# Expert blocks in quarters of the columns, with the activations turned by VectorE in 32x32 blocks

## The reference, cut to what matters

```python
def expert_block(args):
    xblk, e = args
    gu = xblk @ w_gu[e] + b_gu[e]                 # 1024 x 2048: gate | up
    gate, up = jnp.split(gu, 2, axis=-1)
    gate = jnp.minimum(gate, SWIGLU_LIMIT)
    up = jnp.clip(up, -SWIGLU_LIMIT, SWIGLU_LIMIT)
    act = (up + 1.0) * gate * jax.nn.sigmoid(SWIGLU_ALPHA * gate)
    return act @ w_down[e] + b_down[e]            # 1024 x 1024
```

## Time and profile before

| | us |
|---|---|
| median of 3 runs (lowest to highest) | 2428.33 (2425.53 to 2428.96) |
| the profiled execution, own time | 2426.65 |
| its span, first to last instruction | 2424.6 |
| outside the span | 2.05 |
| PE busy | 2286.5 (94%) |
| mean granted clock of TensorE, share of full | 0.974 |

### The profile page before, as it was taken

How to read it: one execution, slowest core, us unless ns; L and a number is a source line. 1 busy time by engine, 2 the same in 40 slices (tenths; PEclk the granted TensorE clock), 3 DMA queues, 4 the chain that set the end, 5 groups by cost and what they waited for, 6 DMA issues and landing times. The chain is left out here.

```text
span 2424.6 us, 40637 instructions
## 1 busy us (share of the span) xinstructions
PE 2286.5 (94%) x17071; PEld 1023.0 (42%) x17071; DVE 686.2 (28%) x1189; ACT 494.4 (20%) x908; POOL 93.7 (4%) x105
## 2 busy tenths in 40 slices
PE   5999869999999999999999993799999998999998
PEld 2434433444444444444444441346445444444443
DVE  1133455111111111111111115102066202365633
ACT  2211222111110111111110111101016202355530
POOL 0000000000000000000000003000000000000000
PEclk9999989999999999999999995899999999999999
DMA  9148439999999999999999965321220121222100
GB/s 352 52 154 310 158 135 382 399 390 392 378 403 397 391 393 393 395 392 390 394 392 398 384 254 174 139 80 70 87 79 8 44 78 44 69 87 87 69 35 35
DMA packets 142024, 561.61 MB, mean 232 GB/s; under 512 B 16217, under 2 KB 31730, under 8 KB 108082
## 3 DMA queue, kind: packets, MB, share of 16 engines
q1 hardware_dynamic: 118662, 512.67, 54.7%
q0 software_dynamic: 9520, 35.26, 4.6%
q10 hardware_dynamic: 13788, 12.93, 1.6%
HBM read 535.77 MB, written 25.03 MB: 231 GB/s over the span
## 5 line engine op out<-in xcount | busy, mean ns | idle before, releaser
L1759 PE MATMUL ps<-ring,xeT 128*32 128x512 f32 x4096 | 491.2, 597 | 2.9 <-ACT xeT L1480 2.9
L1763 PE MATMUL ps<-ring,xeT 128*32 128x256 f32 x4096 | 268.7, 380 | 0.0
L1735 PE MATMUL ps<-ring,aT 128*32 128x512 f32 x2048 | 267.5, 594 | 1.1 <-DVE aT L1638 1.1
L1763 PEld LDWEIGHTS ps<-ring,xeT 128*32 128x32 f32 x4096 | 133.1, 110 | 199.0 <-issue 155.0
L1759 PEld LDWEIGHTS ps<-ring,xeT 128*32 128x32 f32 x4096 | 126.7, 110 | 197.0 <-issue 160.3
L1625 DVE TENSOR_SCALAR gate<-ps 128x768 f32<-128x768 f32 x32 | 30.6, 958 | 547.1 <-PE ps L1763 547.1
L1569 ACT ACTIVATE sig<-gate 128x768 f32<-128x768 f32 x32 | 27.0, 845 | 729.6 <-DVE gate L1625 729.6
L358 PE MATMUL ps<-hT_late,ring 128*128 128x512 f32 x384 | 165.2, 592 | 1.3 <-PEq L1999 1.3
L1740 PE MATMUL ps<-ring,aT 128*32 128x256 f32 x2048 | 157.6, 379 | 0.0
L1740 PEld LDWEIGHTS ps<-ring,aT 128*32 128x32 f32 x2048 | 67.0, 110 | 152.7 <-issue 152.7
L358 PEld LDWEIGHTS ps<-hT_late,ring 128*128 128x128 f32 x384 | 72.9, 190 | 92.9 <-issue 92.9
(11 more groups left out here) (371 smaller groups left out, 2190.0 us busy)
## 6 DMA issues: line engine op xcount, KB each, us to landing
ring<-in_w_gu SPq DMA_DIRECT2D x256, 1024.0 KB, 7.1
ring<-in_w_down SPq DMA_DIRECT2D x128, 1024.0 KB, 7.9
ring<-in_even_w_in SPq DMA_DIRECT2D x18, 1024.0 KB, 6.2
ring<-in_w_ada SPq DMA_DIRECT2D x32, 512.0 KB, 6.4
ring<-in_odd_w_in SPq DMA_DIRECT2D x32, 512.0 KB, 5.3
ring<-in_w_ada SPq DMA_DIRECT2D x8, 1024.0 KB, 21.0
ring<-in_w_in SPq DMA_DIRECT2D x8, 1024.0 KB, 15.8
y_scratch<-ysb ACTq DMA_DIRECT2D x128, 64.0 KB, 4.9
```

Source lines behind the costliest of these rows:

```text
L1735: mm = nc.tensor.matmul(quad(Y0, 2 * q + n), acted(k, q), w[:, kk, n * BANK:(n + 1) * BANK], start=first, stop=last)
L1759: nc.tensor.matmul(quad(2 * b, 2 * q + h), left(q), w[:, at:at + BANK], start=start, stop=stop)
L1763: mm = nc.tensor.matmul(quad(2 * b + 1, c, 256), left(2), w[:, at:at + 256], start=start, stop=stop)
```

## The change

- **gate and up** go by quarters of the columns for all three groups. A quarter c is not a run of columns: `part_columns` takes from gate and from up, of each 128 columns, the 32 at place c, so a matmul streams 2 x 8 runs of 32 columns, 512 in all, which lie 128 apart. A tile has 12 matmuls of 512 columns, three rounds of four strips; group q is in bank q, gate in its first 256 columns, up in the next. Bank 3 is free.
- **The turn of the activations** is one `nc.vector.transpose` of 128x768 from `up` to `turned`, which turns each block of 32x32 where it is. With the new order of columns that gives what `down` needs. PE's 6 transposes and DVE's two copies go. The instruction waits for `down` of the expert before (`y_done`), since that reads `turned`.
- **ids** are written to bank 3 (`IDS`), and `pe_ids` moves from behind the first tile to the end of the step, with a third one before step 0. `down` doesn't wait for `ids_read` any more.
- **The turn of `xe`** has 96 tokens instead of 128, and so has ACT's `act_modulate`.
- **Empty slots** have the id 8192 (`NONE`) and are dropped by the bounds check of the gather; `xe` keeps there what it had.

The diff, cut to its core:

```diff
-        Y0 = 4
+        IDS, Y0 = 3, 4
...
         def dve_ids(dve, S):
-            nc.vector.tensor_scalar(idx[:], ps[:, Y0, 0:1], ps[:, Y0, 1:2], None, ALU.add).then_inc(S.ids_read, 1)
+            nc.vector.tensor_scalar(idx[:], ps[:, IDS, 0:1], ps[:, IDS, 1:2], float(NONE), ALU.add, ALU.add).then_inc(S.ids_read, 1)
...
-                mm = nc.tensor.transpose(ps[:, 6 + k // 4, (k % 4) * P:(k % 4 + 1) * P], src[:, k * P:(k + 1) * P], ident)
+                at = (k % 4) * P
+                mm = nc.tensor.transpose(ps[:, 6 + k // 4, at:at + tokens_], src[0:tokens_, k * P:(k + 1) * P],
+                                         ident[0:tokens_, 0:tokens_])
...
+        FQ = FF // 4
+        def part_columns(w, c):
+            return w.rearrange("p (b j c f) -> p c b j f", b=2, c=4, f=QUAD)[:, c]
+        def part_banks(b):
+            return ps[:, 0:3, b * FQ:(b + 1) * FQ]
...
-            nc.gpsimd.indirect_dma_start(xe[0:CAP, :], None, xn_dram, bass.IndirectOffsetOnAxis(ap=idx[0:CAP, :], axis=0)) \
-                .then_inc(S.gathered, 16)
+            nc.gpsimd.indirect_dma_start(xe[0:CAP, :], None, xn_dram, bass.IndirectOffsetOnAxis(ap=idx[0:CAP, :], axis=0),
+                                         bounds_check=T - 1, oob_is_err=False).then_inc(S.gathered, 16)
...
-                    dve.wait_ge(M.aT_done, e * 2 + 1)
-                    nc.vector.tensor_copy(turned[:, 0:BANK], bank(6)).then_inc(M.aT_read, 1)
-                    dve.wait_ge(M.aT_done, e * 2 + 2)
-                    nc.vector.tensor_copy(turned[:, Q2], bank(7, W - BANK)).then_inc(M.aT_read, 1)
+                    dve.wait_ge(M.act_ready, e + 1)
+                    if not first:
+                        dve.wait_ge(M.y_done, e * 2)
+                    nc.vector.transpose(turned[:, 0:W], up[:, 0:W]).then_inc(M.aT_read, 1)
...
-                for e in range(2):
+                for e in range(3):
...
-                    pe.wait_ge(M.ids_read, e + 3 if not (isinstance(e, int) and e == E) else E + 2)
                     pe.wait_ge(M.y_read, e * 2)
-                    pe.wait_ge(M.aT_read, e * 2)
+                    pe.wait_ge(M.aT_read, e)
...
-                    if q < 2:
-                        at = (k % 4) * P + q * 2 * QUAD + (k // 4) * QUAD
-                    else:
-                        at = BANK + (k % 2) * P + (k // 2) * QUAD
+                    at = q * FQ + k * QUAD
                     return turned[:, at:at + QUAD]
...
-                    for b in range(2):
-                        for q, h in pair_units():
-                            at = b * FF + h * BANK
-                            nc.tensor.matmul(quad(2 * b, 2 * q + h), left(q), w[:, at:at + BANK], start=start, stop=stop)
-                    for b in range(2):
+                    for q in range(3):
                         for c in range(4):
-                            at = b * FF + c * 256
-                            mm = nc.tensor.matmul(quad(2 * b + 1, c, 256), left(2), w[:, at:at + 256], start=start,
-                                                  stop=stop)
+                            mm = nc.tensor.matmul(quad(q, c), left(q), part_columns(w, c), start=start, stop=stop)
...
-                        if k == 0:
-                            pe.wait_ge(M.onehot_ready, e + 3)
-                            if not first:
-                                pe.wait_ge(M.y_read, e * 2)
-                            pe_ids(pe, M)
...
-                    pe.wait_ge(M.act_ready, e + 1)
-                    pe.wait_ge(M.xeT_read, e * 8 + 16)
-                    pe_turn(pe, M.aT_done, up, first=None if first else stream.used, n=W // P)
+                    pe.wait_ge(M.onehot_ready, e + 4)
+                    pe.wait_ge(M.ids_read, e + 3)
+                    pe_ids(pe, M, first=None if first else stream.used)
```

More of the change, by code:

```diff
@@ L35 @@
 EPS = 1e-6
+NONE = 64 * P
 SLOTS, SLOT = 12, 2048
@@ L1438, in dve_ids, with pe_ids, pe_turn @@
         def dve_ids(dve, S):
-            nc.vector.tensor_scalar(idx[:], ps[:, Y0, 0:1], ps[:, Y0, 1:2], None, ALU.add).then_inc(S.ids_read, 1)
+            nc.vector.tensor_scalar(idx[:], ps[:, IDS, 0:1], ps[:, IDS, 1:2], float(NONE), ALU.add, ALU.add).then_inc(S.ids_read, 1)
         def dve_sel(dve, S, column):
             nc.vector.tensor_scalar(sel[:], ones[0:3 * E, :], column, None, ALU.mult).then_inc(S.sel_ready, 1)
-        def pe_ids(pe, S, settle=False):
+        def pe_ids(pe, S, first=None):
             for t in range(NT):
-                mm = nc.tensor.matmul(ps[:, Y0, 0:2], onehot[:, t, :], tokens[:, t, :],
+                mm = nc.tensor.matmul(ps[:, IDS, 0:2], onehot[:, t, :], tokens[:, t, :],
                                       start=t == 0, stop=t == NT - 1)
+                if t == 0 and first:
+                    mm.then_inc(first, 1)
             mm.then_inc(S.ids_done, 1)
-        def pe_turn(pe, signal_, src, first=None, n=KD):
+        def pe_turn(pe, signal_, src, first=None, n=KD, tokens_=P):
             for k in range(n):
-                mm = nc.tensor.transpose(ps[:, 6 + k // 4, (k % 4) * P:(k % 4 + 1) * P], src[:, k * P:(k + 1) * P], ident)
+                at = (k % 4) * P
+                mm = nc.tensor.transpose(ps[:, 6 + k // 4, at:at + tokens_], src[0:tokens_, k * P:(k + 1) * P],
+                                         ident[0:tokens_, 0:tokens_])
                 if k == 0 and first:
@@ L1473, in pool_gather, with act_modulate @@
         def pool_gather(pool, S):
-            nc.gpsimd.indirect_dma_start(xe[0:CAP, :], None, xn_dram, bass.IndirectOffsetOnAxis(ap=idx[0:CAP, :], axis=0)) \
-                .then_inc(S.gathered, 16)
-        def act_modulate(act, S):
+            nc.gpsimd.indirect_dma_start(xe[0:CAP, :], None, xn_dram, bass.IndirectOffsetOnAxis(ap=idx[0:CAP, :], axis=0),
+                                         bounds_check=T - 1, oob_is_err=False).then_inc(S.gathered, 16)
+        def act_modulate(act, S, tokens_=CAP):
             for k in range(KD):
-                nc.scalar.activation(xeT[:, k, :], ps[:, 6 + k // 4, (k % 4) * P:(k % 4 + 1) * P], ACT.Identity,
+                at = (k % 4) * P
+                nc.scalar.activation(xeT[:, k, 0:tokens_], ps[:, 6 + k // 4, at:at + tokens_], ACT.Identity,
                                      bias=mod2[:, k, 0:1], scale=mod2[:, KD + k, 0:1]).then_inc(S.xeT_read, 1)
@@ L1617, in _, with block_step @@
                 rest.on(nc.vector.tensor_tensor(bgu[third], bgu[third], bparts[third], ALU.subtract))
-                def block_step(e):
+                def block_step(e, first):
                     dve.wait_ge(M.ids_done, e + 3)
@@ L1624, in block_step @@
                     dve.wait_ge(M.gate_done, e + 1)
-                    nc.vector.tensor_scalar(gate[:, 0:W], wide(0), 7.0, None, ALU.min).then_inc(M.gu_read, 1)
-                    dve.wait_ge(M.up_done, e + 1)
-                    nc.vector.tensor_scalar(up[:, 0:W], wide(2), 7.0, -7.0, ALU.min, ALU.max).then_inc(M.gu_read, 1)
+                    nc.vector.tensor_scalar(thirds(gate[:]), part_banks(0), 7.0, None, ALU.min).then_inc(M.gu_read, 1)
+                    if not first:
+                        dve.wait_ge(M.aT_read, e)
+                    nc.vector.tensor_scalar(thirds(up[:]), part_banks(1), 7.0, -7.0, ALU.min, ALU.max).then_inc(M.gu_read, 1)
                     dve_sel(dve, M, ident3[:, e + 1:e + 2] if isinstance(e, int) else ident3[:, bass.ds(e + 1, 1)])
@@ L1704, in _ @@
                 with dve.Fori(0, E - 1) as i:
-                    block_step(i + 1)
+                    block_step(i + 1, False)
             @block.tensor
@@ L1747, in acted, with gate_up @@
                 def acted(k, q):
[L1749 to L1752 removed]
+                    at = q * FQ + k * QUAD
                     return turned[:, at:at + QUAD]
[L1755 to L1766 removed]
+                def gate_up(left, w, start, stop):
+                    for q in range(3):
+                        for c in range(4):
+                            mm = nc.tensor.matmul(quad(q, c), left(q), part_columns(w, c), start=start, stop=stop)
                     return mm
@@ L1785, in block_step @@
                     pe.wait_ge(M.sel_ready, e + 1)
-                    gate_up(lambda q: sel[:, 0:QUAD], bparts, False, True, (M.gate_done, M.up_done))
+                    gate_up(lambda q: sel[:, 0:QUAD], bparts[:], False, True).then_inc(M.gate_done, 1)
                     pe.wait_ge(M.gathered, e * 16 + 32)
-                    if not first:
-                        pe.wait_ge(M.aT_read, e * 2)
-                    pe_turn(pe, M.xT_done, xe, first=stream.used)
+                    pe_turn(pe, M.xT_done, xe, first=stream.used, tokens_=CAP)
                     if not first:
                         down(e, m0 + 8, turn)
-                    pe.wait_ge(M.act_ready, e + 1)
-                    pe.wait_ge(M.xeT_read, e * 8 + 16)
-                    pe_turn(pe, M.aT_done, up, first=None if first else stream.used, n=W // P)
```

(3 more changed lines are left out.)

12 lines of the change are left out of this document (6 added, 6 removed).

## The result

The changed kernel takes 2387.69 us (median of 4 runs, 2386.78 to 2389.86), the kernel before 2428.28 beside it. The ratio is 0.9836, 95% interval 0.9819 to 0.9853: 1.6% faster, as forecast (2390, range 2384 to 2403). The profiled execution took 2389.86 us, 2387.9 of it span.

The account below looks back on a forecast made before the run. PE's loop step was taken as the bound. Savings of 28.2 (activations' turn), 6.5 (turns of xe), 2.3 (start) and 1.0 (end) sum to 38.0 us, giving 2390 us, range 2384 to 2403; chance 0.68.

Parts of the forecast that it names:

- The bound: MoE loop: every tile waits for PE and PE for none, so PE's step of 34.04 us is the term that counts.
- The turn of the activations: End of PE's loop step: the turn leaves PE, saving 0.80 us plus 0.14 for entering it, 0.94 us a step.
- ids: Moved from behind the first tile to the step's end: 0.32 us in both places, bounds -0.1 to +0.3 us per step.
- The turn of `xe`: PE's eight turns per step stream 96 columns instead of 128; if streaming sets the pace, 0.21 us saved per step.
- Rival A: The turn of xe keeps its pace because the weight load sets it: 2397 us; chance 0.13.
- DVE: Its new turn of 128x768 is hidden in the loop; 1.0 us taken for the tail, or some 0.2 us less.
- Start: End of step 0 and before: turn gone, ids made while waiting, shorter turns, narrower ACT pieces; 2.3 us saved, give or take 1.5.
- End: Final down waits for DVE's turn instead of the copies, saving 0.7 us, plus 0.3 for the ids: 1.0 us.
- Rival B: Weights become the loop's bound: DMAs stay at 396 GB/s, lag grows 0.8 us a step, PE loses 2 to 12 us; chance 0.07.
- Rival C: Strips' runs of 32 columns slow the stream: 3.1 ns per run loses all 38 us, 6.7 ns gives 2472; chance 0.08.
- Rival D: The loop step's end is bare: branch, waits and ids cost 0.3 us more at 30 boundaries, 2399 us; chance 0.04.
- Outside 357 to 1460 us: Ahead of and behind the experts' stretch, nothing should differ by more than 1 us.

Follow-up runs that it names:

- Experiment 2: The changed kernel with six 128x128 transposes of a constant, which nobody reads, put back on PE behind the ids: 2409.38 us, ratio to before 0.993.
- experiment 3: The changed kernel with the ids directly behind the turn of xe, so the strips are interrupted once per step instead of twice: 2379.9 us, ratio to before 0.9805.
- Experiment 4: The changed kernel with the ids back behind the first tile of gate and up, nothing at the end of a step: 2387.6 us, ratio to before 0.984.
- experiment 1: The changed kernel with the turn of xe over 128 tokens again: 2395.24 us, ratio to before 0.9869.
- experiments 6 and 7: The changed kernel without the third token group in seven of eight gate_up tiles, output wrong: 2365.49 us; the same with empty slots fetching row 0: 2374.63 us.
- experiment 5: The changed kernel with empty slots fetching row 0 again (NONE = 0): 2389.35 us, ratio to before 0.9842.

## Why the prediction was right, by its own steps

**The bound.** PE's step was the term that counts, and stayed it: 220 waits of SP's queue in 600 us, all for PE.

**The sum.** Forecast 38.0 us, measured 38.8 in the rows of the experts: start 1.88 for 2.3; the loop's row 36.02 for 34.8 (30 x 0.94, 30 x 0.21 and the 0.3 of the ids that the forecast booked under the end); the last turn of `xe` to the final `down` 0.90 for 0.9. That it came so near is partly luck: the start gave 0.4 less than forecast, and the ids some 1.1 more, which the forecast had at nothing.

**The turn of the activations, 0.94 us a step.** Right, and so were its two parts, within 0.02. The step got 1.20 us shorter by the traces; without `xe`'s 0.22 and 0.04 of the ids, 0.94 is left. Experiment 2 puts the work alone at 0.72 us, and experiments 3 and 4 put one interruption of the strips at 0.24, together 0.96.

**ids, nothing gained.** The forecast had 0.32 us in both places, and behind `down` 0.32 it is. In the kernel before the first two tiles and the ids took 807.24 - 801.73 = 5.51 us, 0.35 more than two tiles; the forecast didn't count the 0.03 by which the second was late. Experiment 4 separates place from form: in the old place, with the new form of tile and the bank of their own, the step is that of the changed kernel. So the little gain came with the form, not the place; which of the bank, the dropped wait for `y_read` and the twelve equal matmuls it was, no run tells.

**The turn of `xe`, 0.21 us.** Measured 0.22 in the traces and 0.21 by undoing it. Rival A is refuted. The Trainium skill (TensorE: Matmul & The Clock Gate, LDWEIGHTS) ties the load's time to its columns; the load rows agree that 96 rows load no faster than 128 (143 ns both), but 143 is above its estimate of 107, and the pace of the turn follows the 96 columns streamed. The forecast's "a third of that per column" was read too low: by the earlier trace rows it is (143 - 110) / 96 = 0.34 ns against 0.83, two fifths; nothing hangs on it.

**DVE.** The turn takes 978 ns, as taken, and not the 0.2 us less that the forecast had as its other estimate:

```profile
L1658 DVE STREAM_TRANSPOSE aT<-up 128x768 f32<-128x768 f32 x32 | 31.3, 978 | 232.2 <-PE ps L1759 232.2
```

It waits 232 us in all for `down`, and in the loop nobody waits for it.

**Start, 2.3 us.** Measured 1.88. Timeline of PE and ACT of the changed kernel at the end of step 0, which answers to the earlier trace rows:

```profile
388.88 0.88 PE L1458 MATMUL ps<-cst,xe 96*128 96x96 f32 x8
...
389.99 0.84 ACT L1588 ACTIVATE sig<-gate 128x768 f32<-128x768 f32 x1 [14.68 <-DVE gate L1644]
390.74 2.67 ACT L1499 ACTIVATE xeT<-ps,mod 128x96 f32<-128x96 f32 x8
...
393.65 3.01 PE L1774 MATMUL ps<-ring,xeT 128*32 128x512 f32 x16 [3.81 <-ACT xeT L1499]
```

From the turn of `xe` to the tile it is 4.77 us, 5.74 before, so 0.97 gained. The turn of `up` went (0.96), and ACT's eight pieces gained their 0.21 as taken, but they started 0.10 later counted from the start of the turn (1.86 against 1.76), and the tile starts 0.24 behind their end where the turn of `up` started 0.14 behind it. The other 0.91 of the start lies ahead of that.

The step of the forecast that failed here is the 0.2 us for the shorter turn of `xe` at the end of step 0. ACT's pieces don't start when the turn is through but behind ACT's sigmoid, and that waits for DVE's clip of gate. It was so before, too:

```profile
387.11 0.84 ACT L1569 ACTIVATE sig<-gate 128x768 f32<-128x768 f32 x1 [15.09 <-DVE gate L1625]
```

From there to the pieces it is 387.86 - 387.11 = 0.75 us before and 390.74 - 389.99 = 0.75 after, so nothing of a shorter turn could arrive.

The forecast left open how long the half clock would last. The granted clock of the stretch 391.84 to 395.00 us before was 0.53, that of 393.60 to 397.00 after 0.61, and from the first tile of step 1 to the bias 415.97 - 393.65 = 22.32 us went by instead of 20.62, so about 1.7 us are still lost there, outside the 1.88.

**End, 1.0 us.** The table's 0.90 isn't the same quantity. It holds the shorter last turn of `xe` (0.22), which the forecast has in its 31 turns, and it doesn't hold the 0.3 of the ids, which left the loop. So it answers to 0.7 + 0.2 of the forecast, and the part of DVE's turn is 0.68 for 0.7. For the wait of the final `down` the profile now names ACT's copy, not DVE (timeline of the changed kernel, which answers to the earlier trace rows):

```profile
1413.40 0.38 ACT L1600 ACTIVATE ysb<-ps 128x256 f32<-128x256 f32 x1
1413.41 0.98 DVE L1658 STREAM_TRANSPOSE aT<-up 128x768 f32<-128x768 f32 x1 [7.49 <-PE ps L1759]
...
1414.49 1.06 PE L1754 MATMUL ps<-ring,aT 128*32 128x512 f32 x8 [1.03 <-ACT ysb L1600]
```

But ACT's copy ended at 1413.78; DVE's turn ended at 1414.39, 0.10 us ahead of the matmul, and is the likelier release.

**Rival B, the weights.** Half of its mechanism is there: from the issue of a tile to its landing it now takes longer from step to step. Median us to landing (last column) of the tiles issued from 400 to 500 and from 1200 to 1300 us, first of before, then of the changed kernel, then of experiment 3:

```profile
ring<-in_w_gu SPq DMA_DIRECT2D x23, 1024.0 KB, 6.8
...
ring<-in_w_gu SPq DMA_DIRECT2D x23, 1024.0 KB, 7.2
```

```profile
ring<-in_w_gu SPq DMA_DIRECT2D x25, 1024.0 KB, 9.1
...
ring<-in_w_gu SPq DMA_DIRECT2D x24, 1024.0 KB, 15.0
```

```profile
ring<-in_w_gu SPq DMA_DIRECT2D x25, 1024.0 KB, 8.8
...
ring<-in_w_gu SPq DMA_DIRECT2D x24, 1024.0 KB, 19.0
```

In 800 us or 24 steps the lag grew by 0.25 us a step (0.4 in experiment 3, 0.18 in experiment 1 with its step of 33.05, nothing in experiment 2 with its 33.55, and next to nothing before). From 367 to 1420 us PE waited for no tile in any of these, so the other half, the loss, didn't come. The forecast feared 0.8, from 396 GB/s taken as a ceiling; the changed kernel moved 407 in a step. Those 396 were what PE asked for, though the share read 1.01. The sum 13.33 MB in 32.84 us was right, and so was the slack of 22 us that hides it. By these rates the loop would run out of slack at a step about 22 / 31 = 0.7 us below the DMAs' 32.8 to 33.1, at 32.1 to 32.4 us: an estimate from experiments 3, 6 and 7, not run.

**Rival C, the runs.** Refuted for runs of 32, and even 4 columns cost a tile nothing; single ones cost 752 us. So a pattern on the streamed side can slow the stream, but by the places that it touches and not by the run, as the forecast's prices per run had it. The Trainium skill (SBUF — State Buffer, the note on cachelines) asks for two accesses to each 16-byte line; the 32s and 4s agree, the pairs, which meet it, still cost 7% of a tile, and single columns more than double it.

**Rival D, the end of the step.** Refuted: 32.84, and experiment 4 without anything at the end of a step takes the same.

**Outside 357 to 1460 us** the forecast allowed 1 us; it was +3.69 ahead of it and -1.69 behind, in code that is the same but for the first gather. That step was wrong: one execution against one other tells an unchanged stretch of 357 us to 3 or 4 us only. It didn't touch the sum, because that was made in steps of the loop.

## What to carry to other kernels

Where column strips run without a gap, count the interruptions, not only the work in them: full-array work cost 0.24 us more each time it stood alone between strips, so put such pieces side by side (7.8 us here, for an edit that moves four small matmuls). A new pattern on the streamed side was free here in fp32 where each 16 bytes that it touches are used whole (runs of 32 and of 4). And a DMA rate read beside a share of 1.0 is not a ceiling: read whose wait ends last, and take the ceiling from a run in which the DMAs are waited for.

## What the runs showed of the hardware that was not expected

- With four strips at work, a strip needs 1.77 ns for each 16-byte place that it reads, and fp32 reads each twice; the stream hides this while it takes longer itself. fp32 pairs took 2.76 us a tile instead of 2.58, single columns 5.43.
- Leaving and re-entering the strips cost 0.24 us, in both places tried.
- The issue of the same gather on POOL takes 971 ns in the changed kernel and in experiment 5, which drops no row, but 1714 before and 1810 in experiment 1. The bounds check isn't the cause, as experiment 1 has it too. What goes with the length in these traces is the start: in a step of the loop the long ones start 0.02 us (before) and 0.07 us (experiment 1) ahead of DVE's product of `up` and `gate`, the short one 0.28 us ahead, in front of DVE's one-hot; why, no run tells. POOL isn't waited for, so it is worth nothing here. The rows of the changed kernel and of experiment 1 over the run:

```profile
L1492 POOL DMA_INDIRECT xe<-xn_scratch,idx x34 | 33.0, 971 | 24.9 <-issue 16.8 <-DVE idx L1441 8.0
```

```profile
L1492 POOL DMA_INDIRECT xe<-xn_scratch,idx x34 | 61.5, 1810 | 25.1 <-issue 16.8 <-DVE idx L1441 8.4
```

- With the loop's mix of transfers the DMAs gave 405 GB/s when they were the bound (experiments 6 and 7), less than the 420 of the earlier trace rows between 368 and 384 us, and the time to landing grew to 23 us while they did.
